# First attention: scores as three products of rounded halves instead of one float32 product

## What is computed

```
q = rope_tail(rmsnorm(rmsnorm(cq) @ w_uq, q_g))          # 12 heads of 96 = 64 + 32 rotated
k = rope_tail(rmsnorm([ckv @ w_ukv (64), k_rope (32)], k_g))
latent queries (1024):  softmax([q k_ctx, q k_lat] * 96**-0.5) @ [v_ctx, v_lat]
context queries (256):  softmax(q_ctx k_ctx * 96**-0.5) @ v_ctx
```

## Time and profile before

| | |
|---|---|
| median of 3 runs | 3388.43 us (3385.56 to 3391.74) |
| the profiled execution | 3388.43 us, span 3386.7 us |
| PE busy | 3165.7 us (93%) |
| DVE busy | 1582.6 us (47%) |
| ACT busy | 1015.1 us (30%) |
| POOL busy | 464.9 us (14%) |
| mean granted TensorE clock | 0.968 of 2.4 GHz |
| L1239, the scores' matmul records | 480, 232.9 us |

### The profile page before, as it was taken

One profiled execution on the slowest core, in us unless ns is written; L12 is line 12 of the kernel. 1 busy time (PEld: TensorE's weight loads), 2 busy tenths in 40 slices (PEclk: granted clock), 3 DMA queues, 4 the chain that ended last, 5 costly groups with the idle time before them and its releaser, 6 DMA issues. The chain is left out here.

```text
span 3386.7 us, 37587 instructions
## 1 busy us (share of the span) xinstructions
PE 3165.7 (93%) x14242; PEld 2176.1 (64%) x14242; DVE 1582.6 (47%) x1955; ACT 1015.1 (30%) x1363; POOL 464.9 (14%) x367
## 2 busy tenths in 40 slices
PE   5987999999897999999999978879989899999998
PEld 2552333333386888888888856734438688888887
DVE  4123544554425454444444553355533555555554
ACT  3014555555413111111111131025542312221221
POOL 0002555555400000000000000035540000000000
PEclk8987999999998999999999989989999999999999
DMA  9800000000201111111111001000001211111111
GB/s 381 326 36 17 4 3 2 3 3 0 85 27 46 37 37 37 37 37 37 37 37 37 31 13 44 31 16 1 1 13 37 70 44 43 62 43 40 47 62 50
DMA packets 34911, 162.27 MB, mean 48 GB/s; under 512 B 3890, under 2 KB 6706, under 8 KB 24755
## 3 DMA queue, kind: packets, MB, share of 16 engines
q1 hardware_dynamic: 34834, 161.24, 13.3%
HBM read 157.03 MB, written 4.19 MB: 48 GB/s over the span
## 5 line engine op out<-in xcount | busy, mean ns | idle before, releaser
L716 PE MATMUL PS<-f_uh,f_Wh 128*128 128x512 f32 (+1 forms) x1760 | 483.4, 372 | 26.0 <-DVE f_ul L453 25.2
L716 PE MATMUL PS<-f_ul,f_Wh 128*128 128x512 f32 (+1 forms) x1760 | 481.4, 371 | 0.0
L716 PE MATMUL PS<-f_uh,f_Wl 128*128 128x512 f32 (+1 forms) x1760 | 481.3, 371 | 0.0
L866 DVE SCALAR_TENSOR_TENSOR X<-PS,mod,X 128x512 f32<-128x512 f32 (+1 forms) x440 | 305.9, 697 | 308.2 <-PE PS L716 308.2
L716 PEld LDWEIGHTS PS<-f_uh,f_Wh 128*128 128x128 f32 x1760 | 308.2, 188 | 89.6 <-issue 19.4
L716 PE MATMUL PS<-f_gh,f_WDh 128*128 128x512 f32 (+1 forms) x880 | 330.4, 375 | 19.5 <-DVE f_gl L852 17.2
L716 PEld LDWEIGHTS PS<-f_ul,f_Wh 128*128 128x128 f32 x1760 | 308.5, 188 | 59.1
L716 PEld LDWEIGHTS PS<-f_uh,f_Wl 128*128 128x128 f32 x1760 | 308.3, 188 | 59.1
L716 PE MATMUL PS<-f_gl,f_WDh 128*128 128x512 f32 (+1 forms) x880 | 325.3, 370 | 0.0
L716 PE MATMUL PS<-f_gh,f_WDl 128*128 128x512 f32 (+1 forms) x880 | 324.6, 369 | 0.0
L835 DVE SCALAR_TENSOR_TENSOR part<-PS,part,part 128x1023 f32<-128x1023 f32 (+1 forms) x132 | 130.0, 1012 | 329.9 <-ACT part L771 329.9
(11 more groups left out here) (255 smaller groups left out, 4283.0 us busy)
## 6 DMA issues: line engine op xcount, KB each, us to landing
part<-in_mod_w SPq DMA_DIRECT2D x48, 1024.0 KB, 7.4
part<-in_w_up SPq DMA_DIRECT2D x88, 512.0 KB, 3.5
part<-in_w_down SPq DMA_DIRECT2D x22, 1024.0 KB, 5.6
part<-in_w_out SPq DMA_DIRECT2D x16, 512.0 KB, 3.5
X<-in_xT SPq DMA_DIRECT2D x4, 1280.0 KB, 9.8
X<-in_xT SPq DMA_DIRECT2D x1, 5120.0 KB, 16.1
part<-in_wqk SPq DMA_DIRECT2D x8, 512.0 KB, 3.5
out<-X SPq DMA_DIRECT2D x16, 256.0 KB, 2.0
```

What stands on the lines that cost most here:

```text
L716: mm = pe.matmul(ps(bank + c, hi - lo), w_, x_[:, lo:hi], start=f_, stop=l_)
L866: dve.scalar_tensor_tensor(out=X[:, m, lo:hi], in0=ps(DNB[r % 2], hi - lo), scalar=moda(layer, 5, m, 0 if lo < SEQ else 1), in1=X[:, m, lo ...
```

## The change

Queries and keys become two buffers each, high (`qh`, `kh`) and low (`ql`, `kl`), of the rounded type. The normalised slice goes into a float32 buffer `fs` (two, by the parity of the slice). ScalarE rounds it into the high buffer (`high`), VectorE writes the difference into the low one (`low`), and GpSimd's cast now reads the high buffer and waits for `hi`. Preparation gets a step 7, in half-iteration v = 9 ahead of the first part of the maxima; step n now also rounds slice n - 2. Each score product becomes three over all 128 rows. The rows above 96 are cleared once at the start, in eight memsets, each waited for. The row of maxima goes into the high queries alone. `raw`, `sq`, `kx` and `sk` move into the free part of X.

```diff
-            qa = [take(T) for _ in range(2)]
-            ka = [take(T) for _ in range(2)]
+            def halves(kind):
+
+                nonlocal o
+                o += 2 * T
+                return [place(f"h0_{kind}{b}", o - (2 - b) * T, T) for b in range(2)]
+            qh, ql, kh, kl = [halves(kind) for kind in ("qh", "ql", "kh", "kl")]
...
                     if 9 <= v <= 16:
-                        return [("max", v - 9)]
+                        return [("prep", 7)] * (v == 9) + [("max", v - 9)]
...
                     pool.memset(sk[0:64, :], 0.0).then_inc(s["zero"], 1)
                     pool.wait_ge(s["zero"], 1)
+                    for n, x in enumerate((*kh, *kl, *qh, *ql)):
+                        pool.memset(x[96:P, :].bitcast(F32), 0.0).then_inc(s["pad"], 1)
+                        pool.wait_ge(s["pad"], n + 1)
                     for b in range(2):
-                        pool.memset(ka[b][96:97, :], 1.0).then_inc(s["one"], 1)
+                        pool.memset(kh[b][96:97, :].bitcast(F32), 1.0).then_inc(s["one"], 1)
...
-                        pool.wait_ge(s["out"], 6 * p + w + 1)
-                        pool.tensor_copy(dst[0:A_QK, lo:hi], src[0:A_QK, lo:hi]).then_inc(s["cast"], 1)
+                        pool.wait_ge(s["hi"], 6 * p + w + 1)
+                        pool.tensor_copy(dst[0:A_QK, lo:hi], src[0:A_QK, lo:hi].bitcast(F32)).then_inc(s["cast"], 1)
...
+                    def three(out, b, keys, lo, hi):
+
+                        pe.matmul(out, kh[b][:, keys], qh[b][:, lo:hi], start=True, stop=False)
+                        pe.matmul(out, kh[b][:, keys], ql[b][:, lo:hi], start=False, stop=False)
+                        return pe.matmul(out, kl[b][:, keys], qh[b][:, lo:hi], start=False, stop=True)
...
-                                mm = pe.matmul(ps(i % 3, BANK), ka[b][0:97, u * P:(u + 1) * P],
-                                               qa[b][0:97, n * BANK:(n + 1) * BANK], start=True, stop=True)
-                                mm.then_inc(s["S"], 1)
+                                    pe.wait_ge(s["lo"], 6 * h + 6)
+                                three(ps(i % 3, BANK), b, slice(u * P, (u + 1) * P), n * BANK, (n + 1) * BANK)\
+                                    .then_inc(s["S"], 1)
...
+                    def high(p, b, w):
+                        lo, hi = CH[w % 3]
+                        act.wait_ge(s["out"], 6 * p + w + 1)
+                        if isinstance(p, int) and p < 2 and w == 0:
+                            act.wait_ge(s["pad"], 8)
+                        act.activation((kh if w < 3 else qh)[b][0:96, lo:hi], fs[w % 2][0:96, :hi - lo], ACT.Copy)\
+                            .then_inc(s["hi"], 1)
+
                     def step(kind, n, p, b):
                         if kind == "prep":
                             if n < 6:
                                 project(p, n)
-                            if n:
+                            if 0 < n < 7:
                                 inverse(p, n - 1)
+                            if n > 1:
+                                high(p, b, n - 2)
...
+                    def low(p, b, w):
+                        lo, hi = CH[w % 3]
+                        h_, l_ = (kh, kl) if w < 3 else (qh, ql)
+                        dve.wait_ge(s["hi"], 6 * p + w + 1)
+                        dve.tensor_tensor(l_[b][0:96, lo:hi], fs[w % 2][0:96, :hi - lo],
+                                          h_[b][0:96, lo:hi].bitcast(F32), ALU.subtract).then_inc(s["lo"], 1)
```

More of the change, by code:

```diff
@@ L1119, in heads0 @@
             pr = [Xf[:, 2 * T + n * 2 * BANK:2 * T + (n + 1) * 2 * BANK] for n in range(3)]
-            raw = [take(BANK) for _ in range(2)]
-            sq = [take(BANK) for _ in range(2)]
-            kx = take(T)
-            sk = take(T)
+            rest = 2 * T + 6 * BANK
+            kx, sk = [Xf[:, rest + n * T:rest + (n + 1) * T] for n in range(2)]
+            rest += 2 * T
+            raw, sq = [[Xf[:, rest + (2 * x + n) * BANK:rest + (2 * x + n + 1) * BANK] for n in range(2)] for x in range(2)]
+            fs = [take(BANK) for _ in range(2)]
             t1 = take(BANK)
@@ L1145, in heads0 @@
                 s = {n: sem("h0_" + n) for n in
-                     ("tab", "w0", "w1", "one", "zero", "kr", "krc", "krt", "krm", "krp", "krs", "S", "P", "PV", "raw", "rawc",
-                      "sq", "nt", "ln", "rinv", "t1", "ts", "ta", "out", "cast", "vs", "mx", "mc", "mn", "mrow",
+                     ("tab", "w0", "w1", "one", "zero", "pad", "kr", "krc", "krt", "krm", "krp", "krs", "S", "P", "PV", "raw", "rawc",
+                      "sq", "nt", "ln", "rinv", "t1", "ts", "ta", "out", "hi", "lo", "cast", "vs", "mx", "mc", "mn", "mrow",
                       "mr", "o", "bc", "lnr", "rs", "fin", "ad")}
@@ L1199, in cast @@
                         lo, hi = CH[w % 3]
-                        src, dst = (ka[p % 2], kb) if w < 3 else (qa[p % 2], qb)
+                        src, dst = (kh[p % 2], kb) if w < 3 else (qh[p % 2], qb)
                         if w == 0:
                             at_least(pool, "mx", NM * p)
-                        pool.wait_ge(s["out"], 6 * p + w + 1)
-                        pool.tensor_copy(dst[0:A_QK, lo:hi], src[0:A_QK, lo:hi]).then_inc(s["cast"], 1)
+                        pool.wait_ge(s["hi"], 6 * p + w + 1)
+                        pool.tensor_copy(dst[0:A_QK, lo:hi], src[0:A_QK, lo:hi].bitcast(F32)).then_inc(s["cast"], 1)
                     def add(h, u):
@@ L1244, in qk @@
                                     at_least(pe, "P", NS * h + i - 2)
-                                mm = pe.matmul(ps(2, BANK)[:, n * CTX:(n + 1) * CTX],
-                                               ka[b][0:97, (8 + n) * P:(9 + n) * P], qa[b][0:97, SEQ:T],
-                                               start=True, stop=True)
+                                mm = three(ps(2, BANK)[:, n * CTX:(n + 1) * CTX], b, slice((8 + n) * P, (9 + n) * P), SEQ, T)
                                 if n == 1:
@@ L1419, in step @@
                             for lo, hi in ((0, BANK), (BANK, T)):
-                                act.activation(qa[b][96:97, lo:hi], PS[96:97, RB * BANK + lo:RB * BANK + hi], ACT.Copy)\
+                                act.activation(qh[b][96:97, lo:hi], PS[96:97, RB * BANK + lo:RB * BANK + hi], ACT.Copy)\
                                     .then_inc(s["mr"], 1)
@@ L1492, in unit @@
                         norm_ = ps(NB[w % 2], n, slice(0, 96))
+                        f = fs[w % 2][0:96, :n]
+                        at_least(dve, "lo", 6 * p + w - 1)
                         if w < 3:
                             dve.wait_ge(s["rinv"], 6 * p + w + 1)
-                            dve.tensor_tensor(ka[b][0:96, lo:hi], kx[0:96, lo:hi], norm_, ALU.mult)\
+                            dve.tensor_tensor(f, kx[0:96, lo:hi], norm_, ALU.mult)\
                                 .then_inc(s["out"], 1)
@@ L1500, in unit @@
                             dve.wait_ge(s["rinv"], 6 * p + w + 1)
-                            dve.scalar_tensor_tensor(out=qa[b][0:96, lo:hi], in0=x, scalar=g, in1=norm_,
+                            dve.scalar_tensor_tensor(out=f, in0=x, scalar=g, in1=norm_,
                                                      op0=ALU.mult, op1=ALU.mult).then_inc(s["out"], 1)
@@ L1516, in unit @@
                         dve.wait_ge(s["rinv"], 6 * p + w + 1)
-                        dve.tensor_tensor(qa[b][0:96, lo:hi], t1[0:96, :n], norm_, ALU.mult).then_inc(s["out"], 1)
+                        dve.tensor_tensor(f, t1[0:96, :n], norm_, ALU.mult).then_inc(s["out"], 1)
+                    def low(p, b, w):
[4 more added lines that the diff above has]
+                                          h_[b][0:96, lo:hi].bitcast(F32), ALU.subtract).then_inc(s["lo"], 1)
                     def step(kind, n, p, b):
-                        if kind == "prep" and n:
+                        if kind == "prep" and 0 < n < 7:
                             unit(p, b, n - 1)
+                        if kind == "prep" and n > 1:
+                            low(p, b, n - 2)
                         if kind == "max":
```

## The result

| | before | after |
|---|---|---|
| median of 4 runs each | 3387.78 us (3385.56 to 3391.74) | 3433.14 us (3425.98 to 3438.58) |
| ratio after to before, 95% interval | | 1.0131 (1.0110 to 1.0152) |
| the profiled execution | 3388.43 us, span 3386.7 | 3433.44 us, span 3431.7 |
| mean granted TensorE clock | 0.968 | 0.960 |
| VectorE busy | 1582.6 us | 1683.5 us |

The forecast was 3387.6 us, with a range to 3398. The time lies 35 us above that range.

A forecast was written before the change was run, and what follows sets the result against it. TensorE was taken as the bound in attention. Products -43.2, stop at the maxima +24.2, start +8.0 and clock +10.2 sum to -0.8 us against 3388.43, so 3387.6 us, range 3376 to 3398.

The forecast's parts named there:

- The products: Attention scores: three products of rounded halves save 0.36 us per key tile, 43.2 us in all; padding costs nothing.
- The stop behind the late cast: Before each prepared head's maxima: TensorE waits 2.2 us for GpSimd's fifth cast, 24.2 us more over eleven heads.
- The start: Start of the stage: clearing eight pads costs 6.9 us, head 0's maxima 1.1 more, together 8.0 us.
- The clock: Behind the stops before the maxima: 6 of 11 followed by 3.4 us at 1.2 GHz, 10.2 us more.
- my interpolation between 1.64 and 2.46 us: TensorE's stop before the maxima: 2.2 us lies 0.7 of the way from a harmless stop to one losing the clock.
- rival 2: Stops before the maxima: the clock stays up, sum -11.0 us, 3377.4 us; chance 0.30.
- The subtractions: Preparation: six VectorE subtractions per head, some 3 us, fit in its spare time; no term in the sum.
- a cast that lasts 0.6 us longer: GpSimd's cast before the maxima: contention with the subtraction could add 0.6 us x 11 = 7 us; left out.
- Rival 3: First maxima matmul of each head: all 11 stops lose the clock, 3396.1 us, more if the cast is held; chance 0.23.
- VectorE releasing the maxima in mid-run: Sign that the prediction is wrong: during the maxima, TensorE's wait would be ended by VectorE; no size given.

The follow-up runs named there:

- all_three: Changed kernel with all six subtractions on GpSimd, the cast reading `fs` on VectorE's signal, and the ones awaited later: 3355.50 us, ratio 0.9904.
- ones_later: Changed kernel with TensorE's wait for the rows of ones moved from the stage's first matmul to the first score product: 3428.36 us, ratio 1.0128.
- small_adds: Changed kernel with GpSimd's additions of the scores for key tiles 2 to 9 cut to 32 of 1024 columns: 3404.67 us, ratio 1.0046.
- no_sub: Changed kernel with each of VectorE's subtractions cut to 16 columns: 3402.03 us, ratio 1.0039.
- sub_on_gpsimd: Changed kernel with all six subtractions moved from VectorE to GpSimd and a third `fs` buffer: 3409.39 us, ratio 1.0064.
- round_4_earlier: Kernel with subtractions on GpSimd, plus ScalarE's rounding of slice 4 ahead of the logarithm and exponential of slice 5: 3410.48 us, ratio 1.0063.
- cast_from_f32: Changed kernel with GpSimd's cast reading the float32 slice and waiting for VectorE's output, not ScalarE's rounding: 3450.33 us, ratio 1.0180.

## Why the prediction was wrong

**The products: right, slightly too good.** I had 0.36 us per tile. The last head gives 2.93 - 2.60 = 0.33, and the padding is free as the earlier trace rows said. In a preparing head the best case measured, in all_three, saves 50.42 - 47.77 = 2.65 us where I had 3.6. By the distances between the values products, seven tiles of a head are 0.30 to 0.34 us shorter, and the stretch across the change of heads 0.65. The tile behind the start of the maxima is 0.3 longer, and one does not change. Over ten heads the shortfall is 10 x 0.95 = 9.5 us.

**The stop behind the late cast: right.** Predicted 2.2 us by a chain of 4.9 us from the logarithm of slice 4. It ran from 403.72 to 408.68, 4.96 us, with the rounding at 0.61 us each, and the stop was 2.10 in the first head and 2.17 or 2.18 in the other ten.

**The start: right, a little small.** 8.0 us predicted, of which 6.9 for the pads; ones_later puts the pads at 8.0. The first matmul came at 278.21 (predicted 277.5), head 0's maxima 9.0 us later than before and its end 9.4.

**The clock: the term was mis-sized.** I let 6 of 11 stops lose it, at 1.7 us each. Straight behind the forecast stop it fell in just 6 of 11 heads, but the other five lost it behind the second stop, four of them for 6.8 us: 51 us at 0.50 in all, where I had 6 x 3.4 = 20. In the four kernels that have the forecast stop and no second one (small_adds, no_sub, sub_on_gpsimd, round_4_earlier) 41 of 44 stops of 2.1 to 2.7 us lost it. The length alone does not decide, so my interpolation between 1.64 and 2.46 us had no ground: stops of 2.20 and 2.63 us kept the clock, one of 2.10 lost it, and of the stops of 2.17 and 2.18 in the changed kernel five lost it at once and five did not. The Trainium skill (TensorE: Matmul & The Clock Gate, Why this matters for your kernels) asks for gaps under about 3 us. By that rule rival 2 would have been right. The trace disagrees: stops of 2.1 to 2.7 us between dense matmuls were mostly followed by 3.4 us at 0.50. Whether a stop of 1.7 to 2.1 us is harmless in this place no run here shows. My price of 1.7 us was near the truth where nothing else held TensorE up: the heads of sub_on_gpsimd and round_4_earlier that kept the clock were 1.4 to 1.6 us shorter behind the stop, and 3.0 shorter than those with 6.8 us at 0.50. In all_three the gain is 1.1, because 0.4 of it is lost again before the first values product behind the start of the maxima, and in no_sub 0.15, where TensorE at full speed only reached another wait.

**The subtractions: the step that failed.** The prediction said: "some 3 us on each. Both engines have room on average". I put the subtractions at nothing in the sum, and they cost 24 to 31 us (3433.14 against 3409.39 with them on GpSimd and 3402.03 with them cut to 16 columns). The room was there and did not help, because the cost is not in their 3 us. A subtraction that meets an addition waits until the addition is done, two of them met two, and the reductions stand behind them in order. So VectorE, which I had 0.3 us ahead of TensorE in each tile, was up to 5 us behind at the start of the maxima. Its average (24.62 and 22.70 of 45 us) hid where it was late.

I had the right rule and looked at the wrong victim. The earlier trace rows show casts between 391 and 612 ns, so no cast was held there. They say nothing of VectorE's side, nor of GpSimd's long instruction, the addition. In the changed kernel casts were held: 32 of its 72 took 0.86 us or more, though not the fifth of a head, which TensorE waits for (0.61 in all 11). The Trainium skill (GPSIMD Engine Reference, Specifications) says that VectorE operations with two SBUF inputs contend with GpSimd. The traces agree, in both directions: 2.65 us for a subtraction of 256 columns beside an addition, and 1.13 for a cast of 0.61. Priced as a cast that lasts 0.6 us longer, it was 7 us in my text, and I left it out of the sum. The right rows were not those of the casts but these, in the trace of before, which I did not read:

```profile
L1507 DVE SCALAR_TENSOR_TENSOR part<-part,sml,part x24: 896/1004/1111, 291.6 to 847.4; 96x512 f32<-96x512 f32 x24
...
337.82 0.90 DVE L1507 SCALAR_TENSOR_TENSOR part<-part,sml,part 96x512 f32<-96x512 f32 x1
338.34 2.58 POOL L1214 TENSOR_TENSOR X<-X 128x1024 f32<-128x1024 f32 x1 [0.17 <-ACT X L1429]
```

This is the kernel before. L1507 is VectorE's one line in the loop with two SBUF inputs, two instructions per head. All 24 start 0.04 us behind a cast of GpSimd and take 0.90 or 1.11 us, where the same product takes 0.75 in the changed kernel with GpSimd idle (404.37). So VectorE already waited for each of these casts. The instruction at 337.82 runs to 338.72; GpSimd's addition starts in the middle of it and takes 2.58 us where the median is 2.35, so here GpSimd paid 0.2 us. The new instructions in VectorE's queue meet the additions, and then it pays 2 us and more, ahead of work that TensorE waits for.

**The rivals.** Rival 3 named VectorE's subtraction as what might hold the cast, and was on the right side of zero, but its mechanism is not what happened. None of the four had the reductions late (my line on what would prove me wrong did: "VectorE releasing the maxima in mid-run"). In the sum, the ten heads were to gain 4.7 us together (-3.6, + 2.2 and the clock's 0.93 each) and lost 37.4, a miss of 42. Of it 9.5 are the saving's shortfall, 23 are the long heads (four of 4.9 us and one of 3.6 beyond the short ones), and the last 9.5 are the clock and the small waits for held reductions. By the 1.5 us that a loss of the clock cost in sub_on_gpsimd, where I had 0.93 per head, about 6 of these are the clock; that is an estimate, the split was not measured in this kernel.

**What the change would have cost without the hold.** small_adds and no_sub have it nearly removed, and still stand at 1.0046 and 1.0039, 3404.67 and 3402.03 us. Both lie above the range that I gave (3398), so the subtractions are the largest miss and not the only one. The forecast's rest, a stop with its clock in each head and 9 us at the start, eats the saving. It takes both away, as in all_three, to see the products' worth.

## What to carry to other kernels

Before a VectorE instruction with two SBUF inputs is added, look up what GpSimd runs at that moment and how long, then ask what stands behind the new instruction in VectorE's queue. In this kernel its price was the remaining time of GpSimd's instruction, and of the next if that followed without a gap, whatever its own size. Two delays in series hide each other: cast_from_f32 removed one and got slower, sub_on_gpsimd removed the other and stayed slower than before, and only with both gone did the products show their 1%.

## What the runs showed that was not expected

- **The hold is a turn, not a slowdown.** 16 columns took 2.60 us and 256 columns 2.66 beside an addition of 2.35, and 0.17 and 0.41 by themselves. A subtraction that came while GpSimd's cast ran waited for the cast and for the addition straight behind it (408.29, 3.15 us). With one input in PSUM the same subtraction took 0.41 beside the addition.
- **It goes both ways.** The cast took 1.13 in place of 0.61 us when GpSimd had been idle and a subtraction had started 0.03 us earlier.
- **Where the clock fell early, the head was shorter.** 51.8 us with the clock lost at the first stop, 56.8 where it was lost only at the second: by the rows, the late scores kept GpSimd's addition out of VectorE's way. No run tried this by itself.
- **A stop's length does not settle the clock.** Kept after 2.20 and 2.63 us, lost after 2.10, and both after 2.18.
- **The same subtraction of 96x512 takes 1.27 us on GpSimd and 0.68 on VectorE**, and all_three is faster with it on the slower engine, where it delays nothing that TensorE waits for.
